# Moving the key, value and first query projections of a Mamba-and-attention block between its convolution chunks

## What is computed

```python
h = rms_norm(x, norm1_w)
z, xbc, dt_raw, q, k, v = split(h @ w_in)          # 1024, 1536, 32, 1024, 256, 256 columns
xbc = silu(depthwise_conv(xbc))                    # 7 taps over the tokens
xs, B, C = split(xbc)                              # 16 heads of 64; two groups of 128 states
y = ssd(xs, dt, B, C) + flip(ssd(flip ...)) + d_skip * xs
y = rms_norm_by_group(y * silu(z))
a = windowed_gqa(q, k, v, sink, bias)              # 16 heads, 4 of keys and values
x = x + concat(y, a) @ w_out
x = x + (silu(conv3(h2 @ w_gate)) * (h2 @ w_up)) @ w_down,   h2 = rms_norm(x, norm2_w)
```

## Time and profile before

| what | us |
|---|---|
| median of three runs (2322.28 to 2332.11) | 2329.92 |
| the profiled execution's own time | 2326.22 |
| its span, first to last instruction | 2324.4 |
| TensorE busy (share of the span) | 2074.7 (89%) |
| VectorE busy | 1578.8 (68%) |
| ScalarE busy | 987.1 (42%) |
| mean granted TensorE clock | 0.94 |

### The profile page before, as it was taken

One profiled execution on the slowest core, in us unless ns is written; L12 is line 12 of the kernel. 1 busy time (PEld: TensorE's weight loads), 2 busy tenths in 40 slices (PEclk: granted clock), 3 DMA queues, 4 the chain that ended last, 5 costly groups with the idle time before them and its releaser, 6 DMA issues. The chain is left out here.

```text
span 2324.4 us, 37273 instructions
## 1 busy us (share of the span) xinstructions
PE 2074.7 (89%) x15570; PEld 1932.6 (83%) x15570; DVE 1578.8 (68%) x2764; ACT 987.1 (42%) x1423; POOL 16.3 (1%) x36
## 2 busy tenths in 40 slices
PE   2899999889989999998899598887999889798996
PEld 1898889889988988898899587576999786678996
DVE  5787767577668886765755367965666479766664
ACT  1453355344444544553544214444444233444442
POOL 0000000000001000000000000000000000000000
PEclk7899999999998999999999889999999899899998
DMA  5455524448644554344555133221555132123551
GB/s 228 150 200 197 181 109 154 173 165 295 248 146 144 200 199 164 126 165 162 199 205 197 70 145 127 91 71 57 207 197 187 70 129 103 60 91 128 188 192 56
DMA packets 52364, 358.89 MB, mean 154 GB/s; under 512 B 5939, under 2 KB 8499, under 8 KB 9572
## 3 DMA queue, kind: packets, MB, share of 16 engines
q1 hardware_dynamic: 52196, 356.51, 42.7%
HBM read 355.40 MB, written 1.08 MB: 153 GB/s over the span
## 5 line engine op out<-in xcount | busy, mean ns | idle before, releaser
L363 DVE TENSOR_TENSOR w_lo<-raw,w_hi 128x1024 fp32r<-128x1024 f32 x340 | 411.1, 1230 | 251.4 <-ACT w_hi L645 249.7
L418 PE MATMUL projected<-u_hi,w_hi 128*128 128x256 f32 x1728 | 489.6, 283 | 46.3 <-DVE w_lo L363 38.3
L645 ACT ACTIVATE w_hi<-raw 128x1024 fp32r<-128x1024 f32 x340 | 353.2, 1056 | 391.5 <-PE projected L418 327.7
L418 PE MATMUL projected<-u_lo,w_hi 128*128 128x256 f32 x1728 | 483.7, 280 | 0.0
L418 PE MATMUL projected<-u_hi,w_lo 128*128 128x256 f32 x1728 | 483.2, 280 | 0.0
L418 PEld LDWEIGHTS projected<-u_hi,w_hi 128*128 128x128 f32 x1728 | 330.9, 192 | 53.6 <-DVE w_lo L363 39.2
L1365 DVE TENSOR_TENSOR w_lo<-raw,w_hi 128x1024 fp32r<-128x1024 f32 x204 | 245.8, 1222 | 149.1 <-ACT w_hi L1652 148.7
L418 PEld LDWEIGHTS projected<-u_lo,w_hi 128*128 128x128 f32 x1728 | 329.4, 191 | 0.2
L418 PEld LDWEIGHTS projected<-u_hi,w_lo 128*128 128x128 f32 x1728 | 328.8, 190 | 0.0
L1433 PE MATMUL projected<-u_hi,w_hi 128*128 128x256 f32 x992 | 281.3, 284 | 24.3 <-DVE w_lo L1365 24.3
L1433 PE MATMUL projected<-u_lo,w_hi 128*128 128x256 f32 x992 | 279.0, 281 | 0.0
(11 more groups left out here) (348 smaller groups left out, 4210.3 us busy)
## 6 DMA issues: line engine op xcount, KB each, us to landing
raw<-in_stream_dram SPq DMA_DIRECT2D x324, 1024.0 KB, 4.9
w_mod<-in_first_ada_dram SPq DMA_DIRECT2D x8, 1024.0 KB, 13.9
band<-bias_rows SPq DMA_DIRECT2D x1, 3072.0 KB, 14.0
x<-in_xT_dram SPq DMA_DIRECT2D x1, 1024.0 KB
out_dram<-f_sq SPq DMA_DIRECT2D x2, 512.0 KB, 2.6
tri<-in_tri_dram SPq DMA_DIRECT2D x2, 384.0 KB, 5.5
c<-in_c_dram SPq DMA_DIRECT2D x1, 512.0 KB
mask<-in_mask_dram SPq DMA_DIRECT2D x1, 384.0 KB
```

Source lines behind the costliest of these rows:

```text
L363: eng.tensor_tensor(part(w_lo, step, half), raw_half(step, half), part(w_hi, step, half).bitcast(F32), ALU.subtract).then_inc(s_lo_pool if ...
L418: m = pe.matmul(out, a, b, start=start and n == 0, stop=stop and n == 2, **kw)
L645: act.activation(part(w_hi, step, half), raw_half(step, half), ACT.Copy).then_inc(s_hi, 1)
```

## The change

Keys, values and the first query chunk leave the list that is laid among the turns and heads, and are placed one behind each of the last three convolution chunks. The other seven cover chunks are spread anew over the same 23 steps. No instruction is added or removed; the stream of weights in memory has the new order.

```diff
 def plan_second():
     plan = [("rms", 0), ("dt", 0), ("xbc", 4), ("xbc", 5), ("dt_columns", 0), ("xbc", 0), ("cb", 0)]
-    plan += [("xbc", i) for i in range(1, 4)]
+    for i, beside in enumerate((("ak2", 0), ("av2", 0), ("aq2", 0))):
+        plan += [("xbc", i + 1), beside]
     ssd = [("x_turn", i) for i in range(4)] + [("ssd", i) for i in range(SH + VALUES)]
-    plan += interleave([("ak2", 0), ("av2", 0)] + [("aq2", i) for i in range(4)] + [("z", i) for i in range(4)], ssd)
+    plan += interleave([("aq2", i) for i in range(1, 4)] + [("z", i) for i in range(4)], ssd)
```

## The result

| | before | after |
|---|---|---|
| median of the runs, us | 2326.1 (2321.56 to 2332.11, 4 runs) | 2358.0 (2346.64 to 2366.24, 4 runs) |
| ratio, 95% interval | | 1.012 (1.0074 to 1.0165) |
| the profiled execution's own time, us | 2326.22 | 2346.64 |
| span, us | 2324.4 | 2344.9 |

The ratio and its interval come from all runs of both kernels, so they need not equal the quotient of the medians (1.0137 here). The change makes the kernel slower by 1.2%, and by 1.13% (1.0086 to 1.0141) when it was timed again. I had forecast 0.6%: the sign was right, the size half of it, and 2358 lies above my range.

A forecast was written before the change was run, and what follows sets the result against it. VectorE bounds the convolution part, a TensorE chain the middle, both engines the heads. Layer 1's 8.3 us plus layer 2's 5.7 make 14.0 slower: 2326.2 becomes 2340.2, plus 3.7 to the median, 2344 us; range 2330 to 2354.

The forecast's parts named there:

- The start of the keys: Layer 1, behind convolution chunk 1: key projection starts at 1385.94 after 2.5 us of TensorE idleness and takes 7.30 us.
- the pairs: A projection and a convolution chunk cost TensorE 12.6 us, VectorE only 9.8, so the last convolution ends 11.8 us later.
- the copy of chunk 2: Sign in the convolution part: the copy into `zc` near 1400 means the forecast is right, at 1390.6 wrong.
- What lies beside them: Beside the convolution: `w_lo` of values and first query chunk, key copies and transfers, all costed at nothing; slack 0.9 us.
- The middle: Last convolution's end to head 0: 18.5 us where it was 17.3; head 0 at 1439.55, 13.0 us later.
- The heads: Head 0 to gate: two `w_lo` fewer, TensorE with slack, so 75.54 - 4.64 = 70.9 us.
- the case of 12%: Slower rival, 12%: projections behind both gaps take 8.60 us, value or heads' projections also slow; +22.5 us, or 2352.
- The case of the held clock: Rival, 22%: TensorE stays at 2.4 GHz after both short gaps, 3.3 us less per layer; +7.4, or 2337.
- the first gap: TensorE's idle time before the key projection, put at 2.5 us, after which that projection was priced at 7.30 us.
- The faster case: Rival, 9%: convolution keeps its pace, projections fill TensorE's gaps; 6.6 us a layer saved, 2317 in all.

The follow-up runs named there:

- fill_all: Changed kernel plus spare matmuls before the keys (18), before query chunk 1 (32) and three in each head step from 3 on; ratio 1.004 against before.
- fill_gaps: Changed kernel plus spare matmuls only in TensorE's gaps, 18 before the keys and 32 before query chunk 1; ratio 1.0076 against before.
- turns_first: Changed kernel with all four turns and heads steps 0 and 1 directly behind query chunk 0, the seven covers after them; 2333.3 us, ratio 1.0032 against before.
- keys_only: Against the changed kernel, only the keys stay behind convolution chunk 1; values and query chunks return to the list among turns and heads; 2338.96 us, ratio 1.0022 against before.
- one_cover_ahead: Changed kernel with one cover (query chunk 1) ahead of the turns and head 0 in place of two; ratio 1.0066 against before.
- late_heads_only: Changed kernel with its convolution pairing undone: three chunks in a row, then keys, values, query chunk 0; list behind kept; 2356.62 us, ratio 1.0114 against before.
- fill_heads: Changed kernel plus three spare matmuls in each head step from 3 on, none in the gaps before keys and query chunk 1; ratio 1.0084 against before.
- after_again: The changed kernel itself, unaltered, timed and traced a second time; 2356.98 us, ratio 1.0113 against before.

## Why the prediction failed where it did

*The start of the keys, the pairs.* Right. Keys at 1386.0 (1385.94 foreseen), the copy of chunk 2 at 1398.65 (I had 1400.35) and of chunk 3 at 1411.87 (1412.96), the last convolution done at 1419.98 (1421.08). The 1.1 to 1.7 us too many come mostly from the keys of layer 1, which took 5.70 us where I had set 7.30; in layer 2 they took 7.42.

*What lies beside them.* Right in the main: no engine waited for a transfer. The cover of the key copies was thinner than I had it. As the keys of layer 1 ended early, the values' `w_lo`, behind the copies and its `w_hi`, was late, and TensorE waited 0.43 us for it. The rest of VectorE's 2.18 us wait is in the shadow of TensorE.

*The middle.* Right: idle 4.06 us (4.0) before query chunk 1, which takes 7.31 us (7.30), and head 0 at 1438.42 (1439.55). In layer 2 it comes after 64.0 us, 12.6 more than before (I had 11.7), as query chunk 1 takes 8.40.

*The heads.* This term failed. I had 75.54 - 4.64 = 70.9 us for each layer, and reasoned that "TensorE now has slack". Measured: 76.8 and 78.0, so 5.9 and 7.1 us more: 13.0, against the 12.7 us by which the stage (26.7) missed my 14.0. All else together was right to 0.3 us, since 1.2 us too many in layer 1 and 0.9 too few in layer 2 cancel. These 5.9 us are what VectorE's waits among the heads of layer 1 grew by, from 2.6 to 8.5. I took 5.65 us for every projection among them, a price read where TensorE had a projection after every two or three head steps. With five projections there in place of seven the clock fell: in after two of the five in layer 1 and three in layer 2 took 7.2 to 7.7 us. I had this in the case of 12%, "the heads' ones run at a reduced clock as well", but only by 1.65 us a layer.

The check is fill_all, where the clock nearly holds. My sum for a held clock was +7.4: head 0 after 59.8 us and 70.9 us of heads. It measured +11.3: head 0 after 60.2 in both layers, heads of 71.6 and 73.3, the latter with one slow projection. So the order was priced to 4 us, spare work included. (That fill_gaps measured 13.9, beside my 14.0, is chance: my 14.0 holds 6.6 us of slow projections behind the gaps, which fill_gaps does not have, and none among the heads, which it has.) The 15 us between fill_all and after are the clock, or more, as the spare matmuls take time too: 1.7 and 3.8 us ahead of head 0, in layers 1 and 2, and 5.2 and 4.7 us in the heads. Of the clock I had priced the first part and left out the second.

*The rivals.* The case of the held clock (+7.4) did not come: the clock held behind the first gap in layer 1 only, and fell behind the second in both layers and both traces. The faster case was decided where I had put it, at the copy of chunk 2: 1398.65, near 1400 and not 1390.6. Its premise, that TensorE has room beside the convolution, did not hold: the last convolution ended 10.7 us later. But most of that can be had back: with the turns moved up (turns_first) the same pairs cost 0.3%, not 1.1%. The rule of the Trainium skill on interleaving regimes (Perfetto Trace Analysis, Optimization Strategy) gained nothing in any of these orders: no measured version with projections among the convolution chunks is faster than before beyond its interval.

*The scale.* The median moved by 31.9 us and the stage by 26.7, which is the 1.13% of the second timing; what the other 5 us are, no run shows. The profiled execution, at +20.5, was the fastest of the four: the rest of its span was 6.2 us shorter than in the profiled execution of before, for a reason that the last section shows.

## What to carry to other kernels

When covers are moved ahead, look at what then stands first behind the stage that they left: here two projections ahead of head 0 let the second engine idle for 11.5 us, and moving four turns and two head steps up gave back 0.8 of 1.1%. Do not price TensorE's work in a stage that gains slack by rows of the stage that had none; price it at both clock levels, and see what stands between the dense parts. Spare matmuls are a cheap probe for this: a run in which they hold the clock bounds what the order costs, though they take time of their own and, as in the kernel before, can leave the total where it was.

## What the runs showed of the hardware beyond that

*A busy TensorE can lose its clock.* In after, between 1457.5 and 1469.3, it was busy for 11.08 of 11.80 us, and the granted clock was 0.73: in part at 1.2 GHz. The work was four head steps, whose matmuls use 16 rows or 64 columns of the array. With three full matmuls of 0.12 us in each it was 1.00. Before the change, with two or three head steps between projections, the clock was 1.00 in layer 1 from 1438 to 1495 us. That spacing does not hold it always: in layer 2 one projection took 6.3 us, and in keys_only, with the same spacing, two of layer 1 took 6.65.

*Two paces at full clock.* In the feed-forward part, where TensorE is busy without a gap at clock 1.00, the same instructions run at one of two paces. Two windows of 50 us of before (layer 2, then layer 1), and one of after (layer 2):

```profile
2150.00:2200.00 50.00, 50.00 (x427) 50.00 (x427) 31.46 (x40) 23.50 (x27) 0.00 (x0) 1.00 0.53 190
1650.00:1700.00 50.00, 50.00 (x443) 50.00 (x442) 32.81 (x43) 24.52 (x28) 0.00 (x0) 1.00 0.57 200
```

```profile
2160.00:2210.00 50.00, 50.00 (x443) 50.00 (x442) 33.40 (x46) 24.25 (x28) 0.00 (x0) 1.00 0.56 193
```

427 matmuls or 443 in 50 us are 117 and 113 ns for each. The feed-forward part of a layer, from one residual sum to the next, takes 202.3 to 202.5 us or 195.0 to 196.4, and nothing between, in the 26 cases of these thirteen traces (the slow one four times: before and one_cover_ahead in layer 2, late_heads_only and fill_heads in layer 1). The trace of the changed kernel had the quick pace in both layers, and before had the slow one in layer 2 (202.3 us to 195.5), which is 6.8 us and covers the 6.2 between +20.5 and +26.7. The first block has it too: the feed-forward part of its second layer takes 162.2 us in six of the traces and 168.4 to 168.6 in seven, which is 6 of the 8 us by which the stage of after_again stands later. Three such parts together would make a spread of 20 us, which is about what the runs of one kernel have. But each kernel has one trace (the changed one two), so that the pace makes that spread is not shown. What picks the pace, I have not found.
